# Attention weights turned and divided in one product: a scaled unit matrix in place of a division and a transpose

## The reference

```python
def gqa_softmax(q, k, v, bias=None, sink=None):
    s = jnp.einsum("bqhgd,bkhd->bhgqk", q, k).astype(jnp.float32) * HEAD_DIM ** -0.5
    ...
        p = jax.nn.softmax(s, axis=-1)
    return jnp.einsum("bhgqk,bkhd->bqhgd", p.astype(v.dtype), v)
```

```python
    merged = gates[..., :D_MODEL] * (branches[0] @ w_branch[0])
    for i in range(1, N_BRANCH):
        merged = merged + gates[..., i * D_MODEL:(i + 1) * D_MODEL] * (branches[i] @ w_branch[i])
```

## Time and profile before

| | |
|---|---|
| median of 3 runs | 2863.89 us (2862.81 to 2864.13) |
| the profiled execution's own time | 2864.46 us |
| its span | 2862.6 us, granted clock 0.998 |
| TensorE busy | 2722.6 us (95%) |
| VectorE busy | 1350.7 us (47%) |
| ScalarE busy | 436.0 us (15%) |
| DMA | 685.48 MB, mean 239 GB/s |

### The profile page before, as it was taken

How to read it: one execution, slowest core, us unless ns; L and a number is a source line. 1 busy time by engine, 2 the same in 40 slices (tenths; PEclk the granted TensorE clock), 3 DMA queues, 4 the chain that set the end, 5 groups by cost and what they waited for, 6 DMA issues and landing times.

```text
span 2862.6 us, 42389 instructions
## 1 busy us (share of the span) xinstructions
PE 2722.6 (95%) x17586; PEld 1977.2 (69%) x17586; DVE 1350.7 (47%) x2753; ACT 436.0 (15%) x873; POOL 75.4 (3%) x137
## 2 busy tenths in 40 slices
PE   7999999998899899999988998899999999999998
PEld 3544444576666567788644444488788998988997
DVE  3856656442222233785411111179734764843763
ACT  0222220210000012231100000011422211122110
POOL 0100002000000000000100000000000000000000
PEclk9999999999999999999999999999999999999999
DMA  9623339379999985233899999954232444333441
GB/s 377 202 103 122 122 128 356 121 317 421 420 407 421 421 348 165 100 115 148 331 421 421 420 384 421 421 203 160 100 134 104 175 163 147 135 140 116 162 162 45
DMA packets 114765, 685.48 MB, mean 239 GB/s; under 512 B 20752, under 2 KB 22032, under 8 KB 39712
## 3 DMA queue, kind: packets, MB, share of 16 engines
q1 hardware_dynamic: 84144, 600.79, 53.1%
q0 software_dynamic: 16992, 69.54, 6.7%
q10 hardware_dynamic: 13456, 12.59, 1.7%
HBM read 679.46 MB, written 3.41 MB: 239 GB/s over the span
## 4 chain that ended last, share of the span: by engine, by line
PE 37%; DMA 14%; DVE 1%; issue 0%; ACT 0%; SPq 0%; DVEq 0%; ACTq 0%
PE ps L780 14%; DMA ring<-units 14%; PE ps L752 11%; PE ps L1527 2%; PE ps L1346 2%; PE ps L1222 2%; PE ps L1488 1%; DMA early_values<-arena 1%; PE ps L1358 0%; PE ps L1378 0%; PE ps L1088 0%; PE ps L815 0%; PE ps L789 0%; PE ps L798 0%; PE ps L1276 0%
## 5 line engine op out<-in xcount | busy, mean ns | idle before, releaser
L1222 PE MATMUL ps<-ring,arena 128*32 128x256 f32 x2928 | 359.8, 382 | 45.9 <-DMA ring<-units 44.4
L1207 PE MATMUL ps<-ring,arena 128*64 128x256 f32 x2960 | 339.3, 381 | 45.3 <-DMA ring<-units 45.1
L1207 PEld LDWEIGHTS ps<-ring,arena 128*64 128x64 f32 x2960 | 227.0, 137 | 148.7 <-issue 65.5
L1222 PEld LDWEIGHTS ps<-ring,arena 128*32 128x32 f32 x2928 | 175.2, 109 | 222.5 <-DMA ring<-units 90.9
L752 PE MATMUL ps<-h,ring 128*128 128x256 f32 (+1 forms) x992 | 246.0, 408 | 3.2 <-ACT h L1706 2.1
L1047 PE MATMUL ps<-u,ring 128*128 128x512 f32 (+1 forms) x544 | 235.1, 586 | 0.5 <-DVE arena L2345 0.5
L752 PEld LDWEIGHTS ps<-h,ring 128*128 128x128 f32 x992 | 186.7, 190 | 61.3 <-issue 34.7
L1047 PEld LDWEIGHTS ps<-u,ring 128*128 128x128 f32 x544 | 102.6, 191 | 126.7 <-issue 125.1
L2681 DVE COPY u<-ps 32x512 f32<-32x512 f32 (+1 forms) x128 | 70.9, 554 | 209.9 <-PE ps L1222 116.9
L752 PE MATMUL ps<-arena,ring 128*128 128x256 f32 x640 | 139.5, 379 | 1.3 <-DVE arena L3115 1.3
L752 PEld LDWEIGHTS ps<-arena,ring 128*128 128x128 f32 x640 | 121.4, 190 | 18.1 <-DVE arena L3008 1.7
(11 more groups left out here) (501 smaller groups left out, 3958.3 us busy)
## 6 DMA issues: line engine op xcount, KB each, us to landing
ring<-units SPq DMA_DIRECT2D x568, 1024.0 KB, 13.4
slots<-turned_mod POOLq DMA_DIRECT2D x62, 512.0 KB, 5.2
arena<-turned_mod POOLq DMA_DIRECT2D x18, 512.0 KB, 11.2
arena<-quarters ACTq DMA_DIRECT2D x32, 256.0 KB, 2.9
arena<-units POOLq DMA_DIRECT2D x7, 1024.0 KB, 7.2
h<-tokens SPq DMA_DIRECT2D x4, 512.0 KB, 12.2
arena<-neighbours ACTq DMA_DIRECT2D x32, 64.0 KB, 8.8
arena<-tokens ACTq DMA_DIRECT2D x1, 2048.0 KB, 14.2
```

The source lines that it names most:

```text
L1207: last = nc.tensor.matmul(ps[j * slots:(j + 1) * slots, bank, lo:lo + UC], lhsT[:, kt, 0:slots], row_of(w[j], kt), start=(kt == 0), stop=( ...
L1222: last = nc.tensor.matmul(ps[j % 4 * slots:(j % 4 + 1) * slots, banks[j // 4], 0:UC], lhsT[:, kt, 0:slots], row_of(w[j], kt), start=(kt == ...
```

## The change

The division is moved into the turning product. Turning a block is a product with a unit matrix; with a diagonal matrix that holds 1/sum for each query, the same product also divides. So:

- VectorE stops after the reciprocal. The division (line 2462 of before) is gone, and `sums_inverted` is raised in its place.
- ScalarE has a new step `scales(i)` behind `exps(i)` in both layers: two copies of `ident` into `scaled_ident`, each with the scale of its head by partition, in a part of `small` that is free there. It waits for VectorE's reciprocal, and raises `scales_ready`.
- TensorE's `turn` becomes an ordinary `matmul`: the undivided exponentials are the stationary operand, `scaled_ident[:, j, :]` the moving one. It waits for `scales_ready`.

```diff
--- before.py
+++ after.py
@@ -352,6 +352,7 @@
         qk = part(0, 12, 512)
         val = part(6144, 4, 384)
         four = part(7680, 2, 512)
+        scaled_ident = part(0, 2, P, of=small)
         prob = [part(8704, 2, 512), part(9728, 2, 512)]
         gate = part(10752, 2, 512)
         quarter = [part(11776, 2, UC), part(12288, 2, UC)]
@@ -546,7 +547,8 @@
         blocks_ready = sem("product_blocks_ready")
         scores_ready = sem("scores_ready")
         exps_ready = sem("exps_ready")
-        probs_ready = sem("probs_ready")
+        sums_inverted = sem("sums_inverted")
+        scales_ready = sem("diagonal_scales_ready")
         turned = sem("probs_turned")
         turned_kept = sem("turned_kept")
         mixed = sem("values_mixed")
@@ -983,12 +985,12 @@
                     if i == 0 and j == 0:
                         pe.wait_ge(products_taken, products)
                     if j == 0:
-                        pe.wait_ge(probs_ready, before + i + 1)
+                        pe.wait_ge(scales_ready, before + i + 1)
                     if i or j:
                         pe.wait_ge(turned_kept, 2 * (before + i) + j)
                     for kb in range(0 if b < TB else TB, 4):
-                        last = nc.tensor.transpose(ps[:, tb, kb * P:(kb + 1) * P],
-                                                   prob[i % 2][:, j, kb * P:(kb + 1) * P], ident)
+                        last = nc.tensor.matmul(ps[:, tb, kb * P:(kb + 1) * P], prob[i % 2][:, j, kb * P:(kb + 1) * P],
+                                                scaled_ident[:, j, :], start=True, stop=True)
                     last.then_inc(turned, 1)
 
                 def mix(i):
@@ -1760,6 +1762,15 @@
                         last = A(es[:, q:q + 2], es[:, q:q + 2], ACT.Exp)
                     last.then_inc(exps_ready, 1)
 
+                def scales(i):
+                    if i >= len(pairs):
+                        return
+                    q = i % 2 * 2
+                    act.wait_ge(sums_inverted, before + i + 1)
+                    for j in range(2):
+                        last = A(scaled_ident[:, j, :], ident, ACT.Copy, scale=rec[:, q + j:q + j + 1])
+                    last.then_inc(scales_ready, 1)
+
                 def copies(i):
                     if i >= len(pairs):
                         return
@@ -1789,6 +1800,7 @@
                         for j in range(2):
                             i = 2 * chunk + j
                             exps(i)
+                            scales(i)
                             if j == 0:
                                 act.wait_ge(gates_summed, done + 1)
                                 if done:
@@ -1800,6 +1812,7 @@
                             copies(i)
                     elif chunk == 0:
                         exps(chunk)
+                        scales(chunk)
                         act.wait_ge(units_used, at(units_used))
                         act.wait_ge(merged_step, done)
                         next_quarter(chunk)
@@ -2457,9 +2471,7 @@
                     dve.wait_ge(exps_ready, at(exps_ready))
                     if k == 1:
                         link(v.tensor_tensor(sums[:, q:q + 2], sums[:, q:q + 2], es[:, q:q + 2], ALU.add))
-                    link(v.reciprocal(rec[:, q:q + 2], sums[:, q:q + 2]))
-                    pr = prob[i % 2][:, :, lo:512]
-                    v.tensor_tensor(pr, pr, wide(rec[:, q:q + 2], [P, 2, 512 - lo], 2), ALU.mult).then_inc(probs_ready, 1)
+                    v.reciprocal(rec[:, q:q + 2], sums[:, q:q + 2]).then_inc(sums_inverted, 1)
 
                 def keep(i):
                     if i < 0 or i >= len(pairs) or i % 2 == 0:
```

## The result

The changed kernel takes 2887.57 us in the median of four runs (2885.14 to 2888.65), against 2863.91 us before: +23.7 us, a ratio of 1.0082 with a 95% interval of 1.0065 to 1.01. Predicted were 2889.2 us, +25.3, and a range of 2880 to 2896. The kernel is slower, as forecast. The profiled execution took 2885.14 us, 2.4 us less than the median.

A forecast was written before the change was run, and what follows sets the result against it. TensorE was taken to bound the two mixing stages and the weight stream the experts behind them. Records +27.5, tile change +1.4, give-back -3.6 and 0 for the rest made +25.3 us, 2889.2 us, range 2880 to 2896.

The forecast's parts named there:

- The stage is TensorE's, and VectorE's 37.7 us are hidden: Both layers' mixing: TensorE paces it, so removing 36 divisions gains nothing except 1.0 us at the start of layer 1.
- ScalarE's copies are free: Softmaxes of both layers: 72 scale copies of about 0.37 us each fit the cover, value 0 in layer 0.
- a gain on the first wait is lost on the second: Start of layer 1's mixing: 0.4 us gained, then lost behind the table load; value 0, between -1.0 and +0.5.
- Two records in place of one: TensorE's 240 turned blocks: an ordinary fp32 product leaves two records, +0.1144 us a block, +27.5 us.
- The rival of one record: Turning line, both layers: an ordinary product leaves one record here too, +1.6 us, 2865.5 us; chance 4%.
- the one of the tile gaps: Behind each turn: transposes cause the longer gaps at a tile change, 6.3 us would go, 2882.9 us; chance 10%.
- Tile change: Turns right behind a value product: first spacing 0.10 in place of 0.06 us, 34 turns, +1.4 us.
- Give-back: Between a pair's turns in layer 0: longer turns fill TensorE's waits for ScalarE's late copies, -3.6 us.
- All of it reaches the end: Experts behind the mixing: the weight stream starts later by what mixing lost, including layer 0's about 15 us.
- The rival of the hidden layer: Layer 0's share is hidden by the saturated stream behind it; only layer 1's 96 blocks count, 2875.4 us; chance 7%.
- The factor four: Turns on TensorE: transpose mode is four times faster for FP32, a 78.5 us term, 2940.2 us; chance 3%.

The follow-up runs named there:

- the product alone: Kernel before with the turns as ordinary products against the plain unit matrix, VectorE still dividing: 2887.24 us, ratio 1.0076.
- the halves: Two edits of the changed kernel, ordinary products for one head's turn and transposes for the other's: first turn 2871.75 us, second turn 2879.16 us.
- the new order: ScalarE copies the first turned head ahead of the DMA and the gate's tanh in layer 0: on the kernel before 2858.59 us, on the changed kernel 2886.39 us.
- the layers alone: Two edits of the changed kernel, ordinary products in one layer and transposes in the other: in layer 0 2875.96 us, in layer 1 2873.92 us.
- the change again: The changed kernel unedited, run for a second profile and more runs: 2887.84 us.
- second turn only: Changed kernel with ordinary products for the second turn of each pair (head 1) and transposes for the first: 2879.16 us, ratio 1.0055.
- scales and transposes: Changed kernel with its turns as transposes against the plain unit matrix, still waiting for ScalarE's unused scale copies: 2863.76 us, ratio 0.9997.
- layer 0 only: Changed kernel with ordinary products in layer 0 and transposes in layer 1: 2875.96 us, ratio 1.0049.

## Why the prediction was right

- *The stage is TensorE's, and VectorE's 37.7 us are hidden.* Shown: leaving the division out, with nothing in its place, changed nothing (0.9997, 0.9981 to 1.0013).
- *ScalarE's copies are free.* Shown: 0.9997, interval 0.998 to 1.0013. Each takes 0.394 us, close to the 0.37 taken by adding the operand's 0.09 to a plain copy.
- *Start of layer 1: a gain on the first wait is lost on the second.* Shown in the profile after. Its time line there answers to the earlier trace rows:

```profile
1181.24 0.17 DVE L2474 RECIPROCAL small<-small 128x2 f32<-128x2 f32 x1 [1.51 <-ACT arena L1759]
...
1182.15 1.28 ACT L1819 ACT_TABLE_LOAD   x1
...
1182.28 1.13 PE L992 MATMUL ps<-small,arena 128*128 128x128 f32 x8 [0.45 <-ACT small L1771]
...
1183.94 0.59 ACT L1782 ACTIVATE arena<-ps 128x512 f32<-128x512 f32 x1
...
1184.58 1.16 PE L992 MATMUL ps<-small,arena 128*128 128x128 f32 x8 [1.18 <-ACT arena L1782]
```

The table load starts 0.91 us behind the reciprocal, before 0.66; the second turn waits 1.18 us, before 0.90. It starts 0.24 us later behind the reciprocal than before, where 0.4 was taken.

- *Two records in place of one, 0.1144 us a block, 27.5 us.* Shown: 480 records, 0.111 to 0.112 apart, and the product alone makes +23.1 us. The rival of one record falls with it. So does the one of the tile gaps: the value product still starts 0.98 us behind the turn's start, 7 x 0.1117 + 0.20, so the gap of 0.20 stayed with no transpose ahead of it.
- *Tile change, +1.4 us.* Measured 0.05 a time in place of 0.04, 1.7 us.
- *Give-back, -3.6 us.* Shown by the halves, 3.7 us in layer 0, and by the new order, 4.8 - 1.1 = 3.7. That the size fits so well is in part luck. The prediction took the shown waits for all of the lateness, and took them to be filled wholly; in fact 4.8 us were there to be had and 1.1 us of them stayed, and the two errors nearly cancel.
- *All of it reaches the end.* Nearly: the layers alone make +13.0 and +11.0. The rival of the hidden layer asked for 2875.4 and is out, but some 0.9 us seems to vanish between layer 0's mixing and layer 1's, and where it does is open.
- *The factor four* of the Trainium skill's page "TensorE: Matmul & The Clock Gate", section Terms: by it the turns would have cost 78.5 us more. The runs show 2 for blocks of 128x128 in fp32, 0.109 against 0.223 us. The measurement decides.

By its terms as measured, the sum is 27.5 + 1.7 - 3.7 - 0.9 = +24.6, and +23.7 was measured. From the first turn to the end of the span the profiles have +24.0, +24.8 (the change again) and +24.4 (the product alone). The rest, 0.9 us, is within the scatter of single executions, 2885.14 to 2889.44 for the changed kernel.

## What to carry to other kernels

Folding a scale into a transpose by a diagonal matrix was not free here, in fp32 and blocks of 128x128: it traded a record for two, and that was paid in both stages, where TensorE sets the pace, while the division it saved was hidden there. Before moving work off an engine, leave it out and time that: it gives the most that the move can be worth. And where a longer instruction costs less than its length, something is waiting behind it: here a copy that was queued behind a tanh, worth more (-5.3 us) than what the change was about.

## What was not expected of the hardware

- One idle time of about 2 us of TensorE can cost more than itself. In the profiles with a single wait of 2.1 us (no division) and of 1.7 us (second turn only) at the start of layer 1, the next window of 4 us had a granted clock of 0.65 and 0.66. The first made layer 1's stretch 161.5 us where it is 160.2 with scales and transposes, the second cost about 1.5 us. But a wait of 1.7 us was followed by 1.00 throughout in the kernels with scales and transposes and with layer 0 only. At the start of layer 0 the same idle time of 2.4 us was followed by 1.00 (the change again), by 0.79 (the product alone) and by 0.50 (the changed kernel with the new order). So it is no fixed price; what decides which was not tried.
- TensorE's idle time as shown understates a late record: 3.3 us of shown waits went, and the stretch got 4.8 us shorter.
